# Triangle inverses in 64-wide halves, paired scores, moved turns and longer weight rings in a four-layer transformer kernel

## What is computed

```
first kind (twice):
  u = rms_norm(x) @ w_in                      # 1024 -> 10 x 1024
  qa,ka,va,za, qb,kb,vb,zb, ga,gb = split(u)
  ya = dilated_mixture(rope(qa), rope(ka), va) * silu(za)    # 16 heads of 64
  yb = norm(diff_attention(qb, kb, vb)) * silu(zb)           # 8 pairs of heads
  x  = x + (sigmoid(ga)*(ya @ w_proj_a) + sigmoid(gb)*(yb @ w_proj_b)) @ w_out
second kind (twice):
  proj = rmsnorm(x) @ w_in                    # q,k,v,z,b,a of 8 delta heads; sq,sk,sv; ga,gb
  y_a = gated_delta_rule(silu(conv(q,k,v)), g, beta)         # 8 heads of 128
  y_b = sliding_window_attention_with_sink(sq, sk, sv)       # 16 heads of 64
  x = x + rmsnorm((sigmoid(ga)*(y_a@w_up_dn) + sigmoid(gb)*(y_b@w_up_sw)) @ w_o)
  x = x + rmsnorm(square(relu(rmsnorm(x) @ w_ff1)) @ w_ff2)  # 1024 -> 4096 -> 1024
```

## Time and profile before

| | us |
|---|---|
| median of 3 runs | 1938.02 (1937.54 to 1938.33) |
| the profiled execution | 1939.12 |
| its span in the trace | 1937.3 |
| PE busy in the span | 1853.9 |
| DVE, ACT, POOL busy | 1201.1, 921.5, 233.2 |

### The profile page before, as it was taken

One profiled execution on the slowest core, in us unless ns is written; L12 is line 12 of the kernel. 1 busy time (PEld: TensorE's weight loads), 2 busy tenths in 40 slices (PEclk: granted clock), 3 DMA queues, 4 the chain that ended last, 5 costly groups with the idle time before them and its releaser, 6 DMA issues.

```text
span 1937.3 us, 25474 instructions
## 1 busy us (share of the span) xinstructions
PE 1853.9 (96%) x9623; PEld 1523.1 (79%) x9623; DVE 1201.1 (62%) x2323; ACT 921.5 (48%) x1624; POOL 233.2 (12%) x298
## 2 busy tenths in 40 slices
PE   5999999999999999999999989998999999999998
PEld 4877877887787788778888878887777888877887
DVE  4655667666566766676655665556586555665555
ACT  4354365434436645454433454445464333444443
POOL 0301100030030002102213000000201221200000
PEclk9999999999999999998999999999998999999999
DMA  6543534565343456232212445554433221354552
GB/s 242 165 146 114 169 127 164 168 197 170 109 152 131 139 177 206 99 110 81 72 66 87 153 152 196 174 181 164 135 109 95 66 80 66 113 189 155 174 188 95
DMA packets 136817, 270.15 MB, mean 139 GB/s; under 512 B 5500, under 2 KB 8312, under 8 KB 136696
## 3 DMA queue, kind: packets, MB, share of 16 engines
q1 hardware_dynamic: 134820, 265.75, 41.2%
q10 hardware_dynamic: 1876, 2.78, 0.4%
HBM read 267.46 MB, written 1.05 MB: 139 GB/s over the span
## 4 chain that ended last, share of the span: by engine, by line
PE 82%; DVE 9%; ACT 4%; issue 3%; POOL 1%; DMA 1%; SPq 0%; DVEq 0%; POOLq 0%; ACTq 0%
PE bank L374 21%; PE bank L376 21%; PE bank L375 21%; PE bank L398 3%; PE bank L1522 3%; PE bank L1536 2%; DVE buf L1843 2%; PE bank L1535 1%; DVE lo L356 1%; PE bank L1441 1%; DVE scratch L880 1%; PE bank L553 1%; PE bank L545 1%; ACT scratch L670 1%; PE bank L543 1%
## 5 line engine op out<-in xcount | busy, mean ns | idle before, releaser
L374 PE MATMUL bank<-hi,xh 128*128 128x512 f32 (+1 forms) x2016 | 821.5, 407 | 21.8 <-issue 12.0
L376 PE MATMUL bank<-hi,xl 128*128 128x512 f32 (+1 forms) x2016 | 791.4, 393 | 0.0
L375 PE MATMUL bank<-lo,xh 128*128 128x512 f32 (+1 forms) x2016 | 789.1, 391 | 0.0
L348 ACT ACTIVATE hi<-raw 128x1024 fp32r<-128x1024 f32 (+1 forms) x504 | 527.9, 1049 | 341.0 <-PE bank L376 338.8
L356 DVE TENSOR_TENSOR lo<-raw,hi 128x1024 fp32r<-128x1024 f32 (+1 forms) x504 | 610.7, 1225 | 90.1 <-ACT hi L348 89.7
L374 PEld LDWEIGHTS bank<-hi,xh 128*128 128x128 f32 x2016 | 383.6, 190 | 95.8 <-issue 19.3
L376 PEld LDWEIGHTS bank<-hi,xl 128*128 128x128 f32 x2016 | 382.0, 190 | 83.2
L375 PEld LDWEIGHTS bank<-lo,xh 128*128 128x128 f32 x2016 | 384.2, 191 | 68.9
L1740 ACT ACTIVATE scratch<-bank 128x512 f32<-128x512 f32 x48 | 28.7, 599 | 143.5 <-PE bank L1522 143.5
L398 PE MATMUL bank<-square,buf 128*128 128x128 f32 x584 | 87.9, 273 | 7.2 <-POOL buf L918 5.2
L398 PEld LDWEIGHTS bank<-square,buf 128*128 128x128 f32 x584 | 70.8, 140 | 23.8 <-issue 7.6
(11 more groups left out here) (269 smaller groups left out, 1981.9 us busy)
## 6 DMA issues: line engine op xcount, KB each, us to landing
raw<-in_w_in SPq DMA_DIRECT2D x136, 1024.0 KB, 5.0
raw<-in_w_ff SPq DMA_DIRECT2D x64, 1024.0 KB, 5.2
raw<-in_w_proj_a SPq DMA_DIRECT2D x8, 1024.0 KB, 5.0
raw<-in_w_proj_b SPq DMA_DIRECT2D x8, 1024.0 KB, 5.0
raw<-in_w_out SPq DMA_DIRECT2D x8, 1024.0 KB, 5.1
raw<-in_w_up_sw SPq DMA_DIRECT2D x8, 1024.0 KB, 5.0
raw<-in_w_up_dn SPq DMA_DIRECT2D x8, 1024.0 KB, 5.1
raw<-in_w_o SPq DMA_DIRECT2D x8, 1024.0 KB, 5.6
```

What stands on the lines that cost most here:

```text
L348: act.activation(self.hi[g % RING][:, 0:w], src, ACT.Copy).then_inc(self.hi_ready, 1)
L374: pe.matmul(out, xh[:, row, t], self.hi[slot][:, w], start=first, stop=False)
L375: pe.matmul(out, xh[:, row, t], self.lo[slot][:, w], start=False, stop=False)
L376: mm = pe.matmul(out, xl[:, row, t], self.hi[slot][:, w], start=False, stop=last)
```

## The change

- **Inverses.** Levels 0 to 5 stay inside two diagonal blocks of 64x64 of each 128x128 matrix. ACT copies the diagonal blocks of L into `diag` (a new part of step `gram_q`), rows 0 to 63 holding the upper block and rows 64 to 127 the lower, with 64 columns each. Masks (`narrow`), T, TT, Y and lm are 64 columns wide for each matrix; each product is two matmuls of 64x64, one on rows and columns 0 to 63 of the array and one on 64 to 127, alternating, into one bank. DVE subtracts T and TT of the group in one instruction. Level 6 is two products of 64x64 a matrix on one off-diagonal corner and fills `full`. The turn of the first level becomes eight 64x64 matmuls against the identity.
- **Scores** of heads h and h + 1 (h even) are issued in h's step, in the order 128-wide of both, then 256-wide of both.
- **Rings**: 6 `hi` and 5 `lo` pieces, `LEAD` 4, `LO_LEAD` 3; DVE waits for its own slot.
- **Turns**: `ya`'s in banks 2, 3, 0, 1 and other slots; `sk`'s one slot later, `sq`'s behind it, two in one slot; the turns by rows of x one half piece earlier, in all six places.
- The first constants are smaller, one DMA more loads `narrow`, and the DMA scratch is set to 1024.

```diff
-RING = 4
-LEAD = 3
-LO_LEAD = 2
+HI_RING = 6
+LO_RING = 5
+LEAD = 4
+LO_LEAD = 3
...
-            if g >= RING:
-                act.wait_ge(self.pieces_used, g - RING + 1)
+            if g >= HI_RING:
+                act.wait_ge(self.pieces_used, g - HI_RING + 1)
...
+            if g >= LO_RING:
+                dve.wait_ge(self.pieces_used, g - LO_RING + 1)
...
-    p.run(sec("gb", 9), [b + a for a, b in zip(work[4:12], [[], []] + turns("ya") + [[], []])])
+    p.run(sec("gb", 9), [b + a for a, b in zip(work[4:12], [[]] + turns("ya", 0, 2) + [[], []] + turns("ya", 2) + [[]])])
...
-                    b = TURN if arg == "ya" else (TURN, OUT)[turn_at % 2]
+                    b = (2, 3, 0, 1)[f] if arg == "ya" else (TURN, OUT)[turn_at % 2]
...
+                if kind == "a_scores" and arg % 2 == 0:
+                    for h in (arg, arg + 1):
+                        core.free(pe, SCORE[h % 2])
+                        pe.wait_ge(*at("turn_copied", ("ka", h // 4)))
+                    rows = [slice(HD * m, HD * m + HD) for m in range(2)]
+                    for b, r in zip(SCORE, rows):
+                        pe.matmul(B[b][:, 0:P], qT_(qT)[r, arg // 2, 0:P], qT_(kT)[r, arg // 2, 0:P],
+                                  start=True, stop=True)
+                    for b, r, h in zip(SCORE, rows, (arg, arg + 1)):
+                        pe.matmul(B[b][:, P:3 * P], qT_(qT)[r, arg // 2, P:S], qT_(kT)[r, arg // 2, :],
+                                  start=True, stop=True).then_inc(*up("a_scored", h))
...
-        p.run_by_rows(sq[:1], [[], [], [], rows_turns("h", 1) + [("stat_rows", 1), ("rstd",)]], [[], [], [], [("evac", "sq0")]])
+        last = rows_turns("h", 1)
+        p.run_by_rows(sq[:1], [[], [], last, [("stat_rows", 1), ("rstd",)]], [[], [], [], [("evac", "sq0")]])
...
-                         [("turn", "sk", 0)]] + turns("sq", 0, 3) + [turns("sq", 3)[0] + work[0]])
+                         [("turn", "sk", 0)], turns("sq")[0], turns("sq")[1] + turns("sq")[2], turns("sq")[3] + work[0]])
...
+    middle = rows_turns("h2", 0) + rows_turns("h2", 1)
     p.run_by_rows(oo[1:], [y(0, 0, 0) + y(0, 0, 1), [], [], y(0, 1, 0) + [("post_x", 0, 0)]],
-                  [[], [], [], rows_turns("h2", 0) + y(0, 1, 1) + [("post_x", 0, 1), ("mid_stat", 0)]])
+                  [[], [], middle[:2], y(0, 1, 1) + [("post_x", 0, 1), ("mid_stat", 0)]])
...
                 if kind == "level_y":
...
-                    for i, (h, c) in enumerate(HC):
-                        mm = pe.matmul(B[TURN][:, i * P:i * P + P], lm[l % 2][:, h, c, :], tr[g % 2][h][:, c, 0, :],
-                                       start=True, stop=True)
+                    for m in range(4):
+                        cols = slice(m * HALF, (m + 1) * HALF)
+                        if l == LEVELS - 1:
+                            mm = pe.matmul(B[TURN][halves[1], cols], all_of(decay[g % 2])[halves[0], m, HALF:P],
+                                           t_small[g % 2][halves[0], m, :], start=True, stop=True)
+                            continue
+                        for q in halves:
+                            mm = pe.matmul(B[TURN][q, cols], lm[l % 2][q, m, :], t_small[g % 2][q, m, :], start=True, stop=True)
...
+                        for q in halves:
+                            pe.matmul(B[b][q, cols], tt_small[g % 2][q, m, :], yy[q, m, :], start=True, stop=True)
+                        cols = slice((4 + m) * HALF, (5 + m) * HALF)
+                        for q in halves:
+                            mm = pe.matmul(B[b][q, cols], yy[q, m, :], tt_small[g % 2][q, m, :], start=True, stop=True)
...
+                if kind == "gram_q":
+                    act.wait_ge(*at("lower", arg))
+                    for n, q in enumerate(halves):
+                        ins_ = act.activation(diag[arg % 2][q, :, :], all_of(decay[arg % 2])[q, :, q], ACT.Copy)
+                    ins_.then_inc(*up("diag", arg))
...
+                    if l < LEVELS - 2:
+                        ins_ = dve.tensor_tensor(small[g % 2], small[g % 2], bank[:, :], ALU.subtract)
```

More of the change, by code:

```diff
@@ L38 @@
 RAW = 4
-RING = 4
-LEAD = 3
-LO_LEAD = 2
+HI_RING = 6
+LO_RING = 5
+LEAD = 4
+LO_LEAD = 3
 LEVELS = 7
+HALF = P // 2
 def lambda_init(layer):
@@ L373, in multiply @@
                 last = job.stop and n == job.pieces - 1 and kk == k - 1
-                pe.matmul(out, xh[:, row, t], self.hi[slot][:, w], start=first, stop=False)
-                pe.matmul(out, xh[:, row, t], self.lo[slot][:, w], start=False, stop=False)
-                mm = pe.matmul(out, xl[:, row, t], self.hi[slot][:, w], start=False, stop=last)
+                pe.matmul(out, xh[:, row, t], self.hi[slot % HI_RING][:, w], start=first, stop=False)
+                pe.matmul(out, xh[:, row, t], self.lo[slot % LO_RING][:, w], start=False, stop=False)
+                mm = pe.matmul(out, xl[:, row, t], self.hi[slot % HI_RING][:, w], start=False, stop=last)
         if rows[-1] >= k - 1 and blocks[-1] == TB - 1:
@@ L1073, in plan_two @@
     p.run(dn(parts - 2), [[], [("turn", f"f{parts - 1}", 0)], [("turn", f"f{parts - 1}", 1)], []])
-    following = [ahead(rows_turns("h", 0)), ahead([("stat_rows", 0)])] if layer < DEPTH - 1 else [[], []]
+    following = [ahead([what]) for what in rows_turns("h", 0) + [("stat_rows", 0)]] if layer < DEPTH - 1 else [[]] * 3
     p.run_by_rows(dn(parts - 1), [[], y(1, 0, 0), [], y(1, 1, 0) + [("post_x", 1, 0)]],
-                  [[], y(1, 0, 1), [], following[0] + y(1, 1, 1) + [("post_x", 1, 1)] + following[1]])
+                  [[], y(1, 0, 1), following[0] + following[1], y(1, 1, 1) + [("post_x", 1, 1)] + following[2]])
     return p
@@ L1278, in block_two @@
     pair = [(wide[:, 1024:2048], scr[:, 2048:3072])[g] for g in range(2)]
-    tr = [[a[:, 512 * j:512 * j + 512].rearrange("p (c w t) -> p c w t", c=TB, w=2) for j in range(2)] for a in pair]
-    tr_all = [a.rearrange("p (h c w t) -> p (h c) w t", h=2, c=TB, w=2) for a in pair]
-    beta_rows = [four(a[:, 0:512]) for a in pair]
-    yy = region(3072, 512, 2, TB, P)
+    full = [a[:, 0:512].rearrange("p (m t) -> p m t", t=P) for a in pair]
+    small = [a[:, 512:1024] for a in pair]
+    t_small = [mats(a[:, 0:256]) for a in small]
+    tt_small = [mats(a[:, 256:512]) for a in small]
+    beta_rows = [four(a) for a in small]
+    yy = mats(scr[:, 3072:3328])
     state, uu, rr, xx = (region(3584 + 256 * i, 256, 2, P) for i in range(4))
```

140 lines of the change are left out of this document (75 added, 65 removed).

## The result

| | before | after |
|---|---|---|
| median of 4 runs, us | 1937.94 (1937.54 to 1938.33) | 1848.15 (1844.59 to 1850.64) |
| profiled execution | 1939.12 | 1844.59 |
| its span | 1937.3 | 1842.8 |

The ratio is 0.9535 (95% interval 0.9523 to 0.9547): the changed kernel is 89.8 us faster, and its median lies 4.9 under the forecast of 1853. The profiled execution is the shortest of its four, and its span is 94.5 shorter than before.

The account below looks back on a forecast made before the run. The prediction took TensorE's (PE's) own row of instructions, plus the few places where PE stands still, to bound the kernel. Its terms summed to -85.3 from 1939.1, so 1853.8, and 1853 us for a median; the range was 1825 to 1912.

Parts of the forecast that it names:

- Inverses: Triangle inverses in 64-wide corners running side by side: -34 us in sum, with 0.056 us a record and 0.33 a change-over.
- Paired scores: Both attentions: 32 pairs of heads each save 0.99 us, 31.7 in all, with 5 given back in the sliding-window stretch.
- (a): Inverses: corners don't run side by side (+57.6, about 1911 us), or a record stays at 0.112 (1918); chance 0.16.
- (b): Inverses: corners one after another and 0.112 us a record, +179, so 2032 us; chance 0.04 with the half-clock variant.
- level_y's term: Inverses, level_y in 48 places: cheaper records and a vanished wait for DVE's subtraction, 14.0 us saved.
- ya's turns: Differential attention: four other banks, free by then, remove PE's 5.8 us wait for the shared bank, -5.8.
- sk's turn: Each layer: one slot later, 12 more dense matmuls cover the 2.6 us wait for POOL's rotation, -5.2.
- Turns by rows: Six turns of x: issued one half piece earlier, 6 dense matmuls (1.36 us) come in between, -8.2.
- The -3.5 for the rings: Longer rings let ACT and DVE run one piece further ahead; of 4.0 us waits for lo, 3.5 go.
- The clock: Four 3.4 us stretches at granted clock 0.50, at sk's turn and turns by rows, may go: counted -3 us.
- (c): Better: shorter change-over (-13), DVE keeps up in the sliding-window stretch (-5), all four clock dips go (-4); about 1831, chance 0.09.
- (d): Waits for DVE and ACT return in the levels and window attention, +18, so 1872 us; chance 0.19 with mixtures to 1895.

## Why the prediction came out right

Right by its main steps, and closer in the sum than its terms were. The forecast is 85.3 against the profiled execution, and 94.5 came: the clock gave 12.4 more than its term and the rest 3.2 less. That the median is only 4.9 under the forecast, and not 9, is luck: of the four executions the profiled one is the shortest, 3.6 under their median.

- **Paired scores, right.** Two heads cost 1.0. In the first attention 1.6 of the 15.8 goes into a new wait at the second pair (0.55 behind the mask, 0.26 behind ACT, in both layers). The window's give-back, argued from DVE's 17.04 in 19.93, was 5 and is 4.9: the outputs, scores and turns there wait 6.6 more, the squares behind them 1.9 less. The +2 for ACT's SiLUs, for which the prediction had no row, didn't come: with the inverses alone no wait of PE for ACT in the list grows by more than 0.1, and the window attention's places stay within 0.25.
- **Inverses, right in mechanism and size.** The record's price, taken at the lower bound of 0.056 from an uneven pair of distances, is 0.058 (at 0.053 the sum would have moved by 0.003 x 960 = 2.9, not by under 2, as the prediction says); the change-over of 0.33, read from 128-column work, is 0.32. Rivals (a) and (b), +57.6 and +179, are out: the corners overlap fully, in one bank. By the Trainium skill's "TensorEngine Tiling (Array Packing)", Restrictions and Gotchas, different row tiles cannot use one PSUM bank at the same time; for two tiles that differ in row and column and write disjoint partitions the runs disagree, with 1.73 from dense to dense in one bank and in two. level_y's term was short by 2.8, for its wait was mis-sized: it went in 39 of the 48 places, by 0.31 each, where I had counted 34 with 0.27; the other nine places gained 0.07 to 0.15 in all.
- **The cover over level_y, right.** DVE's subtraction is 0.68 and PE doesn't wait for it, save behind a convolution or a gate (5.0, was 5.7). With 1.38 on DVE the waits are back.
- **ya's turns, wrong.** The step that failed is "four other banks, free by then: -5.8". The bank was free, but I didn't follow what stands behind the cut on DVE and ACT, the mask and exponentials of the scores in the same slot. PE came earlier to the next output, and 4.9 of the 5.8 became waits at L604 (6.9, was 2.0).
- **sk's turn, half right.** Its wait went, 2 x 2.6; the turns of sq behind it then met POOL's rotation, 1.24 in one layer and 0.18 in the other, though I had written that their input is there.
- **Turns by rows and rings, right as a sum, wrong as terms.** -8.2 gave -7.8. The -3.5 for the rings is -7.4 when they are taken away with the turns in place: without them the turns would have lost over half of their 8.7 to lo. I priced each against the kernel before, where neither leans on the other.
- **The clock, mis-sized.** -3 was counted, -15.4 came in the profiled execution. The dips were seen in four places; in the trace of before ten stretches at the lower level (a granted clock of 0.50, so 1.2 of 2.4 GHz) stand ahead of the last few microseconds, 47.6 us in all; after there are four, 17.0. One of before and one of after (busy us of PE, PEld, DVE, ACT, POOL; granted clock; DMA):

```profile
1754.00:1757.40 3.40, 3.40 (x10) 2.63 (x9) 1.23 (x1) 1.27 (x2) 0.71 (x1) 0.50 0.02 5
```

```profile
841.20:844.60 3.40, 3.40 (x10) 2.50 (x8) 0.65 (x1) 0.00 (x0) 3.32 (x2) 0.50 0.00 0
```

 The four at sk's turn and at the turns by rows go with the moved turns alone, which backs the 6.8 that they were said to be worth. The others lie behind the squares (32 matmuls of one column each) and in the first levels; some went, and their number changes from run to run of one kernel (0.995 to 0.991 in four runs of the kernel after, 1844.6 to 1850.6). What decides over those was not settled. Through the levels the mean stays at 0.98 in the first of the two layers (877 to 1030) and 0.99 in the second (1437 to 1590), beside 0.99 in both before, so (b) doesn't come by the clock either.
- **(c) and (d).** Of (c) the clock alone came. Of (d) nothing came in the levels, and in the window attention no more than the 4.9 that the sum had given back.

## What to carry to other kernels

Price small work from dense start to dense start: the two numbers of such a reading, record and change-over, priced here a form of instruction that the trace didn't hold. When a wait is removed, follow everything behind the moved step on every engine that does a part of it, not only the resource it waited for. And price parts that lean on each other together: a shorter stop needs buffers that reach over it.

## What the hardware showed that I had not expected

- **Products may start out of the order of the program.** With all products of one corner first, the second corner's first two products run beside the first corner's last two (the rows of x4 at 1036.73 and 1036.85), and level_t takes 0.75 more and not 0.9. The rows don't name the corner; it follows from the lines, as the program has an L1575 of the first corner between its last L1573 and the second corner's first, and the trace shows four records of L1573 ahead of it. "TensorE: Matmul & The Clock Gate" in the Trainium skill, Part 2, says that matmuls stay in program order and only weight loads are pulled ahead; for two tiles that share no rows and columns these rows speak against it: the second corner's first product starts ahead of the first corner's last one.
- **ACT changes function tables on the way to and from a SiLU**, 1.28 for each change, around a SiLU of 1.92: 4.5 us of ACT, and 5.5 from 815.04 to 820.49 with a hi piece of 1.04 between. PE's longest wait in the window attention, 1.44 at 822.11, stands behind it.
- **The clock is worth several microseconds between runs of one kernel**, 8 between those of the paired scores alone (means of 0.983 and 0.990).
